# FFN up projection by seven half-width products with sums on VectorE, and eight modulation panels moved into the attentions

## The reference

```python
def swiglu(x, w_gate, w_up, w_down):          # 256x1024, 1024x2816 twice, 2816x1024
    return (silu(x @ w_gate) * (x @ w_up)) @ w_down

x = layer_norm(ALPHA * x + mix, ln1_g[l], ln1_b[l])
ffn = swiglu(x, w_ffn_gate[l], w_ffn_up[l], w_ffn_down[l])
x = layer_norm(ALPHA * x + ffn, ln2_g[l], ln2_b[l])
```

## Time and profile before

| | |
|---|---|
| median of 3 runs | 2581.43 us (2578.32 to 2584.04) |
| the profiled execution | 2583.22 us, its span 2581.4 us |
| busy: TensorE matmuls, weight loads | 2280.5 us (88%), 1490.7 us (58%) |
| busy: VectorE, ScalarE, GpSimd | 825.8 us (32%), 371.1 us (14%), 38.3 us |
| FFN up stage, layer 0, layer 1 (first L2120 to first L2152) | 304.55 to 466.41 us, 833.23 to 995.12 us |
| L2120, 128x128 weights and 256 columns, 1408 records | 312.8 us busy |
| L2434, VectorE's modulation sums, 224 | 149.7 us busy, 745 ns each |
| mean DMA rate | 255 GB/s over the span |

### The profile page before, as it was taken

The page is one execution under the profiler, slowest core; times in us unless marked ns, Lnnn a source line. Parts: engine busy times, 40 slices in busy tenths (PEclk is TensorE's granted clock), DMA queues, the critical chain, the costliest instruction groups (busy, mean ns, idle before and its releaser), DMA issues.

```text
span 2581.4 us, 37330 instructions
## 1 busy us (share of the span) xinstructions
PE 2280.5 (88%) x16786; PEld 1490.7 (58%) x16786; DVE 825.8 (32%) x1619; ACT 371.1 (14%) x834; POOL 38.3 (1%) x69
## 2 busy tenths in 40 slices
PE   8999999999999999999998997888799987665554
PEld 7788688578786886445655554554464643332322
DVE  1301376423102765533653221222321542111112
ACT  1121000012201000114542000000111420000000
POOL 0000000000000000000000000000000000000000
PEclk9999999999999999999999999999999998878887
DMA  8444587464445884511134999999941089999997
GB/s 308 148 133 160 199 290 261 148 227 151 123 150 168 297 288 147 206 66 35 34 147 192 421 426 426 426 426 426 395 160 64 1 334 390 428 427 427 427 427 300
DMA packets 168384, 658.78 MB, mean 255 GB/s; under 512 B 8310, under 2 KB 55938, under 8 KB 143522
## 3 DMA queue, kind: packets, MB, share of 16 engines
q1 hardware_dynamic: 162544, 639.66, 63.6%
q0 software_dynamic: 5312, 16.59, 2.0%
q10 hardware_dynamic: 370, 0.15, 0.0%
HBM read 655.14 MB, written 1.23 MB: 254 GB/s over the span
## 4 chain that ended last, share of the span: by engine, by line
DMA 27%; PE 26%; DVE 4%; ACT 2%; issue 1%; DVEq 0%; ACTq 0%
DMA ring<-in_moe_w_up 9%; DMA ring<-in_moe_w_gate 9%; DMA ring<-in_moe_w_down 8%; PE psum L491 6%; PE psum L701 5%; PE psum L483 4%; PE psum L627 3%; PE psum L718 2%; PE psum L771 1%; DVE ring L1304 1%; PE psum L731 1%; PE psum L662 1%; ACT ring L939 1%; PE psum L809 1%; PE psum L798 1%; PE psum L1942 1%
## 5 line engine op out<-in xcount | busy, mean ns | idle before, releaser
L701 PE MATMUL psum<-ring,arena 128*32 128x256 f32 x5888 | 384.4, 417 | 160.9 <-DMA ring<-in_moe_w_up 82.7
L701 PEld LDWEIGHTS psum<-ring,arena 128*32 128x32 f32 x5888 | 209.0, 118 | 333.0 <-issue 142.4
L2120 PE MATMUL psum<-ht,ring 128*128 128x256 f32 x1408 | 312.8, 383 | 2.1 <-ACT ht L2189 2.1
L2120 PEld LDWEIGHTS psum<-ht,ring 128*128 128x128 f32 x1408 | 267.9, 192 | 45.5 <-issue 9.1
L718 PE MATMUL psum<-ring,lnp 128*32 128x256 f32 x3072 | 193.8, 406 | 66.9 <-DMA ring<-in_moe_w_down 62.3
L491 PE MATMUL psum<-ring,ht 128*128 128x512 f32 x448 | 196.1, 594 | 0.0
L718 PEld LDWEIGHTS psum<-ring,lnp 128*32 128x32 f32 x3072 | 103.7, 116 | 154.7 <-DMA ring<-in_moe_w_down 49.1
L1496 DVE TENSOR_TENSOR arena<-psum,spare 32x512 f32<-32x512 f32 (+1 forms) x128 | 70.9, 554 | 361.3 <-PE psum L718 360.0
L2041 PE MATMUL psum<-ht,ring 128*128 128x256 f32 x768 | 166.7, 379 | 0.0
L2041 PEld LDWEIGHTS psum<-ht,ring 128*128 128x128 f32 x768 | 145.9, 190 | 20.7 <-issue 1.0
L2434 DVE SCALAR_TENSOR_TENSOR arena<-ring,arena 128x512 f32<-128x512 f32 x224 | 149.7, 745 | 0.0
(11 more groups left out here) (408 smaller groups left out, 2075.6 us busy)
## 6 DMA issues: line engine op xcount, KB each, us to landing
ring<-in_moe_w_down SPq DMA_DIRECT2D x64, 2048.0 KB
ring<-in_moe_w_gate SPq DMA_DIRECT2D x62, 2048.0 KB
ring<-in_moe_w_up SPq DMA_DIRECT2D x60, 2048.0 KB
ring<-in_w_in SPq DMA_DIRECT2D x52, 1024.0 KB
ring<-in_ada_w SPq DMA_DIRECT2D x48, 1024.0 KB
ring<-in_w_ffn_gate SPq DMA_DIRECT2D x22, 1024.0 KB
ring<-in_w_ffn_up SPq DMA_DIRECT2D x22, 1024.0 KB
ring<-in_w_ffn_down SPq DMA_DIRECT2D x20, 1024.0 KB
```

The source lines that it names most:

```text
L701: last = mm(bank[32 * j:32 * j + 32, SPLIT * m:SPLIT * m + SPLIT], (x_last if layer else x_four)[:, k, e % 4, SLOTS * m:SLOTS * m + SLOTS] ...
L2120: last = mm(bank[:, SEQ * u:SEQ * u + SEQ], slot[:, k, SEQ * u + P * h:SEQ * u + P * h + P], xT[:, k, :], start=k == 0, stop=k == KT - 1)
```

## The change

The up stage is cut into 2x2 blocks as the down stage is: the weights of a pair into halves of the features (tiles 0 to 3, 4 to 7) and its two 128-column tiles, `xT` into halves of the features and of the tokens. Seven products of 4 tiles replace eight, for gate and up alike; each matmul has 128x128 weights and 128 columns. Four products take sums of weights (`ff_weight_sums`: three into single buffers, one in place in the ring slot), four take sums of x (`x_sums_made`, once a layer, one of them in place in `xT`), both made by VectorE. The products lie in four banks (A: 5 and 6, B: 3 and 7, C: 1 and 2, D: 4), from which VectorE combines gate and up (`ff_parts`), after ScalarE has copied product 1 out. SiLU and product now take the whole pair at once (512 columns). The weight sums of pair p+1 wait until product 3 of pair p is done.

The eight modulation panels stand in the ring's order among the attentions' panels, their sums and small matmuls at eight places there. The SiLU of the conditioning inputs and the transposes of the parameters come after the first b panel. `ada_acc` lies in `spare`, bank 7 is held from the start of the layer, so seven banks rotate until it is given back. POOL's loads of the second norm's parameters and of the context come later, the context after the last pair. The down stage no longer waits for all of `hid` before it opens its banks, and takes in each of its first four panels product by product instead of pair by pair. The same numbers are computed in another order of additions.

```diff
+def ff_banks(p):
+    banks = (("A", (5, 6)), ("B", (3, 7)), ("C", (1, 2)), ("D", (4,)))
+    return [banks[i] for i in (2, 1, 0, 3)] if p == 0 else banks
...
     for b in range(3):
-        layer += [("b", b, 0), ("b", b, 1), R]
+        layer += [("b", b, 0), ("b", b, 1), R] + ([("par",)] if b == 0 else [EV])
...
-    for p in range(FFN_TILES // 2):
-        layer += [(BankPlan.HOLD, BANKS - 1, ("adaG",))] * (p == 1)
-        layer += [("ff", 2 * p)] + [EV] * (1 <= p < 8) + [("adaG",), R] * (p == 8) + [("ff", 2 * p + 1), R]
-        layer += [("adaT", p)] * (p < 2) + [("adaGT",)] * (p == 9)
+    for p in range(PAIRS):
+        for name, _ in ff_banks(p):
+            layer += [("ff", p, name)] + [BankPlan.TICK] * (p > 0 and name == "A")
+        layer += [R] + [("adaT", p)] * (p < 2)
...
-    ADA_PANEL, DOWN_PANEL = 22, 40
+    ADA_PANELS, FF_PANEL, DOWN_PANEL = (2, 4, 7, 10, 13, 16, 17, 20), 29, 40
...
-                for b in range(3):
-                    project_T(("b", b), panel(l, HALF), xT)
+                project_T(("b", 0), panel(l, HALF), xT)
                 pe.wait_ge(par_loaded, 4 * 16)
...
+                project_T(("b", 1), panel(l, HALF), xT)
+                ada_rows_of(0)
+                project_T(("b", 2), panel(l, HALF), xT)
+                ada_rows_of(1)
...
+                def ff_factors(c, k, u, slot):
+                    w = slot[:, 4 * (c in (2, 4)) + k, SEQ * u:SEQ * u + SEQ]
+                    left = ff_sums[c][:, k, u, :] if c in ff_sums else w[:, P:SEQ] if c in (4, 7) else w[:, 0:P]
+                    if c in x_sums:
+                        return left, x_sums[c][:, k, :]
+                    return left, xT[:, 4 * (c in (2, 3)) + k, P * (c in (3, 5)):P * (c in (3, 5)) + P]
...
-                    for h in range(2):
-                        if h and 1 <= p <= 8:
-                            ada_rows_of(p - 1)
-                        bank = open_bank(pe, "layer", ("ff", 2 * p + h), l)
-                        for u in range(2):
-                            for k in range(KT):
-                                last = mm(bank[:, SEQ * u:SEQ * u + SEQ], slot[:, k, SEQ * u + P * h:SEQ * u + P * h + P],
-                                          xT[:, k, :], start=k == 0, stop=k == KT - 1)
+                    for name, two in ff_banks(p):
+                        bank = open_bank(pe, "layer", ("ff", p, name), l)
+                        for j, c in enumerate(two):
+                            if c in (5, 6, 3, 7):
+                                pe.wait_ge(ff_sums_ready, 4 * (l * PAIRS + p) + {5: 1, 6: 2, 3: 3, 7: 4}[c])
+                            if p == 0 and c in (7, 5, 6, 4):
+                                pe.wait_ge(x_sums_ready, 4 * l + {7: 1, 5: 2, 6: 3, 4: 4}[c])
+                            for u in range(2):
+                                for k in range(4):
+                                    left, right = ff_factors(c, k, u, slot)
+                                    a = SEQ * j + P * u
+                                    last = mm(bank[:, a:a + P], left, right, start=k == 0, stop=k == 3)
+                            if c == 3 and p > 0:
+                                last.then_inc(pe_done, 1)
                         last.then_inc(pe_done, 1)
...
-                wait_emptied(pe, "layer", ("ff", FFN_TILES - 1), l)
...
+                def ff_weight_sums(p):
+                    n_panel = FF_PANEL + p
...
+                    if p:
+                        dve.wait_ge(pe_done, banks.full("layer", ("ff", p - 1, "A"), l) + (p > 1))
+                    w = view(ring[:, n_panel % RING, :], KT, 2, 2, P)
+                    a11, a21, a12, a22 = (w[:, 4 * c:4 * c + 4, :, r, :] for c in range(2) for r in range(2))
+                    s1, s2, s4 = ff_sums[5], ff_sums[6], ff_sums[3]
...
+                    TTo(s1, a21, a22, ALU.add).then_inc(ff_sums_ready, 1)
...
+                    TTo(s2, s1, a11, ALU.subtract).then_inc(ff_sums_ready, 1)
...
+                    TTo(s4, a12, s2, ALU.subtract).then_inc(ff_sums_ready, 1)
+                    TTo(a21, a11, a21, ALU.subtract).then_inc(ff_sums_ready, 1)
...
+                def ff_parts(p):
+                    dve.wait_ge(ff_1_ready, l * PAIRS + p + 1)
...
+                    step(TTo(ff_16, ff_1, part[6], ALU.add))
+                    step(TTo(ff_167, ff_16, part[7], ALU.add))
+                    TTo(ff[:, :, 1, P:SEQ], ff_167, part[5], ALU.add)
+                    TTo(ff_16, ff_16, part[5], ALU.add).then_inc(freed["A"], 1)
+                    TTo(ff[:, :, 0, 0:P], ff_1, part[2], ALU.add).then_inc(freed["C"], 1)
+                    wait_emptied(dve, "layer", ("ff", p, "A"), l)
+                    TTo(ff[:, :, 0, P:SEQ], ff_16, part[3], ALU.add).then_inc(freed["B"], 1)
+                    TTo(ff[:, :, 1, 0:P], ff_167, part[4], ALU.subtract).then_inc(freed["D"], 1)
...
+                x_sums_made()
+                for p in range(PAIRS):
+                    if p + 1 < PAIRS:
+                        ff_weight_sums(p + 1)
+                    else:
                         turned(0, 8)
                         down_sums(0)
+                    if p:
+                        ff_product(p - 1)
+                    ff_parts(p)
```

More of the change, by code:

```diff
@@ L1974, in _, with ada_rows_of @@
                 transpose_x("xT", x_ready)
-                for b in range(3):
-                    project_T(("b", b), panel(l, HALF), xT)
+                def ada_rows_of(i):
+                    state["panel"] += 1
+                    bank = open_bank(pe, "layer", ("adaG",), l) if i == 0 else psum[:, banks.bank("layer", ("adaG",)), :]
+                    pe.wait_ge(ada_ready, l * 8 + (i + 1))
+                    for q in range(4):
+                        last = mm(bank[32 * q:32 * q + 32, 0:SEQ], one_pad[:, 7 - i:39 - i],
+                                  ada_acc[:, i % 2, q // 2, SEQ * (q % 2):SEQ * (q % 2) + SEQ], start=i == 0, stop=i == 7)
+                    last.then_inc(pe_done, 1)
+                project_T(("b", 0), panel(l, HALF), xT)
                 pe.wait_ge(par_loaded, 4 * 16)
@@ L2070, in _ @@
                 project_T(("mb",), panel(l, D), yb, tiles=4, k_tiles=4)
+                ada_rows_of(5)
+                ada_rows_of(6)
                 gate_panels("a")
+                ada_rows_of(7)
                 wait_emptied(pe, "layer", ("pva", 3), l)
                 project_T(("ma",), panel(l, D), ya, tiles=4, k_tiles=4)
+                wait_emptied(pe, "layer", ("adaG",), l)
+                transposes("layer", ("adaGT",), [ada_g[:, P * j:P * j + P] for j in range(2)], l)
                 gate_panels("c")
@@ L2097, in ada_T @@
                     transposes("layer", ("adaT", p), [ada_rows[:, p % 2, :]], l)
-                def ada_rows_of(i):
-                    bank = open_bank(pe, "layer", ("adaG",), l) if i == 0 else psum[:, banks.bank("layer", ("adaG",)), :]
-                    pe.wait_ge(ada_ready, l * 8 + (i + 1))
-                    for q in range(4):
-                        last = mm(bank[32 * q:32 * q + 32, 0:SEQ], one_pad[:, 7 - i:39 - i],
-                                  ada_acc[:, i % 2, q // 2, SEQ * (q % 2):SEQ * (q % 2) + SEQ], start=i == 0, stop=i == 7)
-                    last.then_inc(pe_done, 1)
                 ada(0)
@@ L2124, in _ @@
                         ada_T(p)
-                    if p == 9:
-                        wait_emptied(pe, "layer", ("adaG",), l)
-                        transposes("layer", ("adaGT",), [ada_g[:, P * j:P * j + P] for j in range(2)], l)
-                down = {c: open_bank(pe, "layer", ("dn", c), l) for c in SEVEN}
-                wait_emptied(pe, "layer", ("ff", FFN_TILES - 1), l)
                 def factors(c, i, slot, sums):
@@ new lines, in x_sums_made @@
+                def x_sums_made():
+                    for t in range(TT):
+                        for m in range(2):
+                            wait_emptied(dve, "layer", ("x1T", t, m), l)
+                    b11, b12, b21, b22 = (xT[:, 4 * r:4 * r + 4, P * c:P * c + P] for r in range(2) for c in range(2))
+                    for n, (out, in0, in1) in enumerate(((x_sums[7], b22, b12), (b12, b12, b11), (x_sums[6], b22, b12),
+                                                         (x_sums[4], x_sums[6], b21))):
+                        TTo(out, in0, in1, ALU.subtract).then_inc(x_sums_ready, 1)
+                        dve.wait_ge(x_sums_ready, 4 * l + (n + 1))
@@ L2439, in turned @@
                 def turned(a, b):
-                    for f in range(2 * a, 2 * b):
-                        wait_emptied(dve, "layer", ("ff", f), l)
                     h4 = hid.rearrange("p (i c) n -> p i c n", c=2)[:, a:b]
```

212 lines of the change are left out of this document (126 added, 86 removed).

## The result

| | us, median | runs | against the kernel before, same chip |
|---|---|---|---|
| before | 2582.73 (2578.32 to 2585.43) | 4 | |
| changed | 2546.75 (2544.22 to 2549.17) | 4 | 0.9862 [0.9844, 0.9881] |

The direction was right, the forecast gain over a quarter too small. The profiled execution took 2548.3 us, span 2546.5.

The account below looks back on a forecast made before the run. TensorE was taken to set the up stage, with the DMA-bound part moving with its work. Products 23.5 plus end idle 2.9 make 26.4 us, 0.4 kept for small losses: 2555.4 us for the median, range 2549 to 2570.

Parts of the forecast that it names:

- Rival 2: Up stage: seven wait points a pair on TensorE break the stream, gain only 14 us, 2568 us; chance 0.15.
- rival 3: Attentions: panel margins fail by 3 us per layer, 6 us come back, 2561 us; chance 0.09.
- rival 4: Up stage: a record at 0.122 to 0.127 us, no gain to be seen, 2576 to 2587 us; chance 0.05.
- rival 1: Up stage: the weight load sets the pace, 0.154 us a record, 2653 us, losing from 0.125; chance 0.06.
- I take 0.1144: Up stage: price in us of a 128-column record, from the value projection's 32; pair 12.8 us, 23.5 us gained.
- the low end, 0.1138: Up stage: cheapest record price in us, a pair of 12.75; with no losses it was to give 2552 us.
- The 129-column stretch: Second block: 40 matmuls in 4.56 us, 0.114 each, taken to include bank waits, as evidence for the record price.
- the slow starts: Up stage start: first pair 15.54 us in place of 13.88, 1.7 us; range widened 3 us in case less is lost.
- The stage: Up stage length: about 143 us in place of 162, layer 0's down stage starting about 13 us earlier.
- The end idle: Before the down projection: TensorE's 1.44 us wait for VectorE's last product goes, 2.9 us in two layers.
- the margin of 0.2: Up stage end: VectorE's first down sums done 12.6 us after pair 9, pair 10 ending at 12.8.
- The moved panels: Up stage to attentions: row matmuls 5.6 us out, 5.6 in per layer, 0 net; first panel's margin 1.3 us.

Follow-up runs that it names:

- moved_only: The changed kernel with the up stage and down-stage entry of before, only the eight modulation panels moved: 2580.7 us, ratio 0.9986 against the kernel before.
- before_again: The kernel before, unchanged, run for a second trace: 2577.61 us.
- cols64: The changed kernel with only the first 64 of 128 token columns in every up-stage matmul, 128x128 weight loads kept: 2797.48 us.
- down_waits: The changed kernel, but TensorE waits before the down stage until VectorE frees the last pair's last bank: 2557.88 us, ratio 0.9896 against the kernel before.
- vector_load: The changed kernel with sixteen more 512-element VectorE instructions in each of the first eight up-stage pairs: 2679.66 us, ratio 1.0378 against the kernel before.

## Why the prediction was right and wrong

**Right: the mechanism.** TensorE's records are the stage, VectorE fits beside them, and the DMA-bound part moves with TensorE's work. TensorE is busy 138.0 of 138.1 us and no releaser stands inside the stage. Rival 2 fell (no step at a wait is over 0.113 us), rival 3 (no idle before the row matmuls) and rival 4 (a record far below 0.122); rival 1 had the right limit and the wrong price.

**Wrong: the price of a record**, the step "I take 0.1144", and with it the low end, 0.1138. It measured 0.1117; against the same 13.88 a pair gains 1.37 and not 1.07, over 22 pairs 30.1 us and not 23.5. This alone takes the forecast from 2555.4 to 2548.8, below the range. The rows had the answer. In the earlier trace rows I divided 3.66 us by 32 records. The last of the 32 steps leads to a group of another shape, and in the same trace it is longer. The timeline of the kernel before, from 607.14 us (both rows are cut by the window):

```profile
607.14 0.50 PE L2001 MATMUL psum<-ring,ht 128*128 128x128 f32 x3
607.56 0.37 PE L2010 MATMUL psum<-arena 64*128 64x128 f32 x1
```

Three records start at 607.14, 607.25 and 607.36, the next group at 607.56: a last step of 0.20. The 31 steps before it take 603.90 to 607.36, 0.1116 each. The 129-column stretch has its border too: its 39 steps are 0.1116 each (1223.13 to 1227.48) and the last, to L552, 0.21, so what I called bank waits in it were not there. Neither end of the price was a bound from below: a stretch of n records has n - 1 steps of its own, and a border of 0.1 us spread over 32 looked like 3% of the price.

The same slip stood in the pair before, and there it helped. The 96 records of the earlier trace rows have one step of 0.32, the first behind the row matmuls; the others are 0.216. An undisturbed pair is 13.82, as moved_only shows, not 13.88, so the products gain 22 x 1.32 = 29.0 us, and the rest left with the row matmuls (6.4 us a layer with their borders, where 5.6 and two transposes were forecast).

The low end of the range has an error of its own. A record at 0.1138 gives 22 x 1.13 + 2.9 = 27.8 us and so 2553.6, not 2552; without it the range would have begun at 2550.6, still further from the result.

**Wrong: the slow starts**, kept on both sides at 1.66 us a layer, with 3 us of the range for them. They differ between executions, and the up stages of the changed kernel had none in six. That gives up to 3.3 us more. With the 6.6 of the products it makes 26 into 36. That the two sums meet so well is partly luck: the pair's border takes 1.2 back, the end idle 0.6, the panels and edges below add 2.6, and from mix to the end one kernel scatters by 5 us. Finer than that the sum can't be closed.

**The stage**, forecast 143 us: 138.15. Without the slow start 141.3 was forecast, and 11 x 0.3 of pairs is the rest. Layer 0's down stage starts 19.7 us earlier (466.41 to 446.74), where 13 was forecast.

**The end idle**, 2.9 us: gone but for 0.28 a layer, 2.3 us. The pairs became shorter than forecast and VectorE's work did not, which used up the margin of 0.2.

**The moved panels**, 0 net: 6.4 us out and 4.9 in for each layer, so a gain of 3 us, within what moved_only measured (1.0 to 6.2). The margin of the first panel was 1.3 us, as worked out. What I missed is the edge, 10.5 in place of 9.2: the last modulation columns and the next layer's first x transposes now share a bank, and a wait of 2.96 us appeared at a place that the change doesn't touch.

In sum, from before_again to the changed kernel, until mix: start 0.4, stages 44.1 (2 x 22.06), attentions -8.9, edge -1.4, second edge (15.9 to 14.9) 1.0; together 35.2 of 35.3 us seen (1071.65 to 1036.37). Against the two other traces of the kernel before, which have the slow starts, it is 40.9 and 40.2.

## What to carry to other kernels

Take the time per instruction from the distance between starts inside one group, n - 1 steps for n records, and keep its borders apart: a few per cent on a term that occurs thousands of times was nearly a fifth of this gain (6.6 of 36 us). Apply it to the price before as well as to the price after: the pair of before had the same flaw. Cutting matmuls from 256 to 128 columns was nearly free here, since a record then takes 0.1117 us against half of 0.216; at 64 columns it takes no less, and in cols64 the clock fell as well. Waits of 3.25 and of 5 to 7 us on a dense TensorE cost 1.5 to 1.8 us more each at half clock, so work for a slower engine is moved out of the stage that it would stall, together with the cut.

## What the runs showed of the hardware

- The clock can halve for a whole stage on an engine that counts as busy: 64-column f32 matmuls behind 128x128 loads got 0.50 for 250 us, after 2 us at full clock.
- A wait of 3.25 us of TensorE was followed by 3.4 us at half clock in both layers of down_waits, from 1 us behind the wait on; in vector_load the clock fell within a wait of 6.42 us (at 379.3 of 376.8 to 383.2) and rose 3 us behind it. Waits of 1.04 us before the up stages were followed by it in some traces and not in others, those of 1.44 us before the down stages in none.
- Load and stream of an f32 record overlap: behind 128 weight columns the step is 0.1117 with 128 columns and with 64, behind 64 weight columns 0.109. The records' own durations (0.275 for the matmul, 0.19 for the load) say nothing of either.
- From matmuls with 128 weight columns to a group with 64 or 32, the step is about 0.1 us longer (0.20 for 0.11 at 607.36, 0.31 for 0.22 at 370.75 in the kernel before); to a transpose with 128 it is not (0.22 at 450.56).
